# Tokens, meta tokens, norm gains and a low rank weight laid out by partition before the launch, in a two-block transformer kernel

## What is computed

```
h = concatenate([meta, x], axis=1)                   # 16 + 256 tokens, 1024 wide
hn = rmsnorm(h, norm_mix[0])
h = h + gla_mixer(hn, gla_w_in, gla_w_a1, gla_w_a2, gla_b_a, gla_g_out, gla_w_out)
...                                                  # ffn, sparse attention, ffn
h = concatenate([zeros, meta_2, x], axis=1)          # the second stack, x from the first
```

## Time and profile before

| | us |
|---|---|
| median of 3 runs | 1350.13 (1350.03 to 1351.98) |
| the profiled execution | 1350.41 |
| its span, first to last instruction | 1348.6 |
| TensorE matmul busy in it | 1341.5 (99%) |
| TensorE weight load busy | 1281.3 (95%) |
| VectorE, ScalarE, GpSimd busy | 1009.2, 708.1, 296.7 |
| DMA, mean over the span | 170 GB/s |

### The profile page before, as it was taken

One profiled execution on the slowest core, in us unless ns is written; L12 is line 12 of the kernel. 1 busy time (PEld: TensorE's weight loads), 2 busy tenths in 40 slices (PEclk: granted clock), 3 DMA queues, 4 the chain that ended last, 5 costly groups with the idle time before them and its releaser, 6 DMA issues.

```text
span 1348.6 us, 24729 instructions
## 1 busy us (share of the span) xinstructions
PE 1341.5 (99%) x9873; PEld 1281.3 (95%) x9873; DVE 1009.2 (75%) x1613; ACT 708.1 (53%) x1167; POOL 296.7 (22%) x313
## 2 busy tenths in 40 slices
PE   9999999999999999999999999999999999999998
PEld 9999999999999888899999999999999999988886
DVE  6788766655997988888877876766557885898843
ACT  7565544444756555544444664544445565655543
POOL 1136000023152000132366744000022533120000
PEclk9999999999999999999999999999999999999999
DMA  8334665665443655555443455555554653566552
GB/s 280 126 125 157 193 188 186 194 187 161 135 159 128 218 190 191 170 200 187 160 139 126 154 187 160 187 168 177 172 172 145 191 157 127 168 202 192 193 183 77
DMA packets 220457, 229.72 MB, mean 170 GB/s; under 512 B 13664, under 2 KB 207704, under 8 KB 220344
## 3 DMA queue, kind: packets, MB, share of 16 engines
q1 hardware_dynamic: 219232, 226.24, 52.7%
q10 hardware_dynamic: 1112, 1.90, 0.6%
HBM read 226.80 MB, written 1.33 MB: 169 GB/s over the span
## 4 chain that ended last, share of the span: by engine, by line
PE 99%; DMA 0%; issue 0%; DVE 0%; ACT 0%; ACTq 0%; DVEq 0%
PE ps L605 28%; PE ps L603 21%; PE ps L601 20%; PE ps L598 14%; PE ps L1163 2%; PE ps L1162 2%; PE ps L1164 2%; PE ps L664 1%; PE ps L666 1%; PE ps L665 1%; PE ps L932 1%; PE ps L802 1%; PE ps L1007 1%; PE ps L790 0%; PE ps L1095 0%; PE ps L889 0%
## 5 line engine op out<-in xcount | busy, mean ns | idle before, releaser
L1204 ACT ACTIVATE uh<-raw 128x1024 fp32r<-128x1024 f32 (+4 forms) x452 | 446.7, 999 | 433.5 <-PE ps L605 372.9
L1800 DVE TENSOR_TENSOR ul<-raw,uh 128x1024 fp32r<-128x1024 f32 (+3 forms) x448 | 528.3, 1187 | 130.0 <-PE ps L605 82.1
L605 PE MATMUL ps<-xx,ul 128*128 128x272 f32 (+1 forms) x2136 | 603.1, 282 | 0.0
L601 PE MATMUL ps<-xx,uh 128*128 128x272 f32 (+1 forms) x1448 | 419.1, 289 | 0.0
L603 PE MATMUL ps<-xx,uh 128*128 128x272 f32 (+1 forms) x1448 | 414.9, 287 | 0.0
L605 PEld LDWEIGHTS ps<-xx,ul 128*128 128x128 f32 x2136 | 402.3, 188 | 0.0
L601 PEld LDWEIGHTS ps<-xx,uh 128*128 128x128 f32 x1448 | 272.4, 188 | 3.0 <-issue 1.7
L603 PEld LDWEIGHTS ps<-xx,uh 128*128 128x128 f32 x1448 | 272.6, 188 | 0.8
L605 PE MATMUL ps<-aa,ul 128*128 128x272 f32 (+1 forms) x920 | 260.7, 283 | 0.0
L598 PE MATMUL ps<-xx,uh 128*128 128x512 f32 x704 | 244.7, 393 | 0.0
L601 PE MATMUL ps<-aa,uh 128*128 128x272 f32 (+1 forms) x788 | 226.7, 288 | 0.0
(11 more groups left out here) (343 smaller groups left out, 1645.6 us busy)
## 6 DMA issues: line engine op xcount, KB each, us to landing
raw<-in_ffn_w SPq DMA_DIRECT2D x62, 1024.0 KB, 5.3
raw<-in_ffn_w_in SPq DMA_DIRECT2D x44, 1024.0 KB, 5.2
raw<-in_ret_w_in SPq DMA_DIRECT2D x24, 1024.0 KB, 5.1
raw<-in_ffn_w_out SPq DMA_DIRECT2D x16, 1024.0 KB, 5.7
raw<-in_gla_w_in SPq DMA_DIRECT2D x11, 1024.0 KB, 5.1
raw<-in_ret_w_o SPq DMA_DIRECT2D x8, 1024.0 KB, 5.2
raw<-in_dsa_w_in SPq DMA_DIRECT2D x7, 1024.0 KB, 5.5
raw<-in_ffn_w_out SPq DMA_DIRECT2D x8, 768.0 KB, 5.0
```

What stands on the lines that cost most here:

```text
L601: e.matmul(in_turns(ps[:, 0:n1 - n0]), hi[:, k, :], in_turns(x.hi[:, k0 + j, n0:n1]), start=first and j == 0, stop=False)
L605: i = e.matmul(in_turns(ps[:, 0:n1 - n0]), lo[:, k, :], in_turns(x.hi[:, k0 + j, n0:n1]), start=False, stop=last and j == len(ks) - 1)
L1204: i = e.activation(unit_hi(u)[:, :, cols], a, ACT.Copy)
L1800: i = e.tensor_tensor(unit_lo(u)[:, :, cols], a, unit_hi(u)[:, :, cols].bitcast(F32), ALU.subtract)
```

## The change

The host now hands over arrays that are already laid out by partition: `tokens` ([128, 8, 272], meta tokens and `x` together), `meta_2` ([128, 8, 16]), `gla_w_a1` ([128, 8, 16]) and all `gains` ([128, 120]). The transposes, the staging buffers and the copies out of PSUM go. `h` is loaded directly, in four pairs of chunks: 0 and 1 by SP behind the low rank weight, 2 and 3 by SP behind the first half of slab 1, 4 to 7 by ScalarE's queue. The squares for the norm are taken in channel order, on GpSimd for chunks 0 to 3 and on ScalarE for 4 to 7; VectorE adds them up in one reduction, TensorE sums over partitions (`total`), now after five chunks of unit 2, ScalarE takes the root, VectorE the reciprocal. Ten warm-up matmuls run instead of six. Cut to its core:

```diff
 TensorE
-            warm(5)
-            ps = small("gain0", "D")
...
-                for n in (1, 2):
-                    i = turned(ps, k, n)
...
+            warm(10)
...
-            chunk(("gk", 1), "D", x, 0, T)
-            ps = small(("n", 0), "D")
-            w.wait_ge(s_diag, 3)
-            done(e.matmul(ps[:, 0:T], ones[:, :], g_diag[:, P - NM:3 * P], start=True, stop=True), ("n", 0))
+            gk1 = lin.take(w, ("gk", 1), "D")
+            product(gk1, x, 0, T, 0, True, False, range(5))
+            total(("n", 0), "A", s_first, 1, ssq[0], T)
+            product(gk1, x, 0, T, 5, False, True, range(5, KC))
...
-            product(gk2, x, 0, T, 0, True, False, range(4))
-            ps = small("gain1", "D")
-            w.wait_ge(s_row, 16 * (len(ROWS) - 1))
-            done(e.transpose(ps[:, 0:NG], grow[0:NG, :], ident[0:NG, 0:NG]), "gain1")
+            product(gk2, x, 0, T, 0, True, False, range(6))
             gate(0)
             gate(1)
...
-                        i = e.transpose(ps[:, k * NM:(k + 1) * NM], r_stage[0:NM, k * P:(k + 1) * P], ident[0:NM, 0:NM])
 ScalarE
+            e.dma_start(gains[:, 0:NG], A["gains"]).then_inc(s_gain, 16)
+            for j in (2, 3):
+                e.dma_start(h[:, 2 * j:2 * j + 2, :], A["tokens"][:, 2 * j:2 * j + 2, :]).then_inc(s_h[j], 16)
             w.wait_ge(s_const, 4)
             table(ACT.Sqrt)
+            hi()
+            w.wait_ge(s_gain, 16)
+            for k in range(KC):
+                x_hi(0, k, 0, G(gcol["norm_mix"] + k), (s_h[k // 2], 16))
             w.wait_ge(s_gz, 1)
             for r in (0, 32):
                 e.dma_start(g_a2[r:r + 16, :], A["gla_w_a2"][0]).then_inc(s_a2, 16)
...
+            hi_in_halves()
             hi()
+            for j in (2, 3):
+                e.activation(tmps[:, 2 * j - 4:2 * j - 2, :], h[:, 2 * j:2 * j + 2, :], ACT.Square).then_inc(s_sq[0], 1)
             hi()
+            root(("n", 0), float(D), eps6, rbc[:, :])
             table(ACT.Exp)
 VectorE
+            lo()
             for k in range(KC):
+                x_lo(0, k, 0, G(gcol["norm_mix"] + k))
             lo()
             lo()
+            w.wait_ge(s_ssq[0], 7)
+            w.wait_ge(s_sq[0], 2)
+            e.tensor_reduce(ssq[0][:, :], tmps[:, 0:5, :].rearrange("p k n -> p n k"), AX, ALU.add).then_inc(s_first, 1)
             lo()
...
             w.wait_ge(*aux.emptied(("n", 0)))
+            e.reciprocal(rbc[:, :], rbc[:, :]).then_inc(s_first, 1)
 GpSimd
+            for k in range(4):
+                src, sq = h[:, k, :], total if k == 0 else tmp[5] if k == 1 else sqt[:, k % 2, :]
+                w.wait_ge(s_h[k // 2], 16)
+                e.tensor_tensor(sq, src, src, ALU.mult).then_inc(s_ssq[0], 1)
+                if k:
+                    w.wait_ge(s_ssq[0], 2 * k)
+                    e.tensor_tensor(total, total, sq, ALU.add).then_inc(s_ssq[0], 1)
 SP
-            e.dma_start(cst[:, 0:P], A["c_tab"][:, 0:P]).then_inc(s_id, 16)
...
                     if s == units[HALVED][0]:
                         e.dma_start(to[:, 0:4, :], src[:, 0:4, :]).then_inc(s_raw_half, 16)
+                        e.dma_start(h[:, 2:4, :], A["tokens"][:, 2:4, :]).then_inc(s_h[1], 16)
                         to, src = to[:, 4:8, :], src[:, 4:8, :]
                     e.dma_start(to, src).then_inc(s_raw[s % NRAW], 16)
+                if s == 0:
+                    e.dma_start(h[:, 0:2, :], A["tokens"][:, 0:2, :]).then_inc(s_h[0], 16)
```

More of the change, by code:

```diff
@@ L506, in build @@
         s_raw_half, s_hi_half, s_lo_half = sem("s_raw_half"), sem("s_hi_half"), sem("s_lo_half")
[L508 to L511, removed]
+        s_const, s_tab, s_gain, s_meta, s_first, s_a2 = (
+            sem(n) for n in ("s_const", "s_tab", "s_gain", "s_meta", "s_first", "s_a2"))
+        s_h = [sem(f"s_h{i}") for i in range(KC // 2)]
         s_gx = sem("s_gx")
@@ L973, in _ @@
             rows("d", y_dsa, [5, 6, 7])
-            def new_meta(t):
-                if t == 8:
-                    ps = small("meta", "A")
-                    w.wait_ge(s_rstage, 16)
-                    for k in range(KC):
-                        i = e.transpose(ps[:, k * NM:(k + 1) * NM], r_stage[0:NM, k * P:(k + 1) * P], ident[0:NM, 0:NM])
-                    done(i, "meta")
-            ffn(1, NM, new_meta)
+            ffn(1, NM, lambda t: None)
             x = norm_x(4)
@@ L1206, in hi, with hi_in_halves @@
                 u += 1
-            def hi_in_halves(between):
+            def hi_in_halves():
                 nonlocal u
@@ L1566, in new_meta @@
                 if t == 5:
-                    e.dma_start(r_stage[0:NM, :], A["meta_2"]).then_inc(s_rstage, 16)
+                    w.wait_ge(s_xl[2], KC)
+                    w.wait_ge(s_ssq[2], 15)
+                    e.dma_start(h[:, :, 0:NM], A["meta_2"]).then_inc(s_meta, 16)
                     for hd in range(2):
                         e.dma_start(r_dk[hd], A["c_dec"][:, hd * DW:(hd + 1) * DW]).then_inc(s_dk[hd], 16)
-                if t == 9:
-                    w.wait_ge(*aux.full("meta"))
-                    e.activation(h[:, :, 0:NM], aux.bank("meta")[:, 0:KC * NM].rearrange("p (k n) -> p k n", k=KC),
-                                 ACT.Copy).then_inc(aux.empties("meta", "A"), 1)
             ffn(1, NM, new_meta)
@@ L2242, in meta_square @@
                 if t == 12:
-                    w.wait_ge(*aux.emptied("meta"))
+                    w.wait_ge(s_meta, 16)
                     e.tensor_tensor(r_sqm, m, m, ALU.mult).then_inc(s_metasq, 1)
@@ L2802, in bias_part @@
                     [LB, NR], [NR * (LB + 1), 8], [1, NKEY[b]]])).then_inc(s_bias, 16)
-            e.dma_start(cst[:, 0:P], A["c_tab"][:, 0:P]).then_inc(s_id, 16)
-            for half in range(2):
-                cols = slice(half * 512, half * 512 + 512)
-                for b in range(2):
-                    e.dma_start(g_stage[:, 1 + b, cols], A["x"][0, b * P:(b + 1) * P, cols]).then_inc(s_x[half], 16)
             for s, (loads, made) in enumerate(slabs):
                 if s == NRAW:
-                    for r0, n, src in rows[1:]:
-                        e.dma_start(grow[r0:r0 + n, :], src).then_inc(s_row, 16)
-                    e.dma_start(cst[:, P:C_END], A["c_tab"][:, P:C_END]).then_inc(s_tab, 16)
+                    e.dma_start(cst[:, :], A["c_tab"]).then_inc(s_tab, 16)
                 if s >= NRAW:
@@ L2894 @@
     named = [(n, np.ascontiguousarray(inputs[n])) for n in _INS]
+    given = {n: np.asarray(a) for n, a in inputs.items()}
+    gains = np.concatenate([given[n].reshape(-1, P) for n, _ in ROWS], axis=0)
+    named += [("tokens", in_columns(np.concatenate([given["meta"], given["x"][0]], axis=0).T)),
+              ("meta_2", in_columns(given["meta_2"].T)), ("gla_w_a1", in_columns(given["gla_w_a1"][0])),
+              ("gains", np.ascontiguousarray(gains.T))]
     for name, a in named + [("c_tab", tab), ("c_hot", hot), ("c_dec", dec)]:
```

104 lines of the change are left out of this document (17 added, 87 removed).

## The result

| | before | after |
|---|---|---|
| median | 1350.36 us (20 runs, 1350.03 to 1351.98) | 1352.51 us (20 runs, 1351.72 to 1354.23) |
| profiled execution, its span | 1350.41, 1348.6 | 1352.3, 1350.5 |

The ratio is 1.0017, with a 95% interval of 1.001 to 1.0023: the changed kernel is 2.1 us slower, which is real, and less than the 0.2% named ahead. The forecast was 1351.8 us, 1.7 over the three runs known then, and no change that can be told.

The account below looks back on a forecast made before the run. Bound: gapless TensorE, so only unit 1's start and TensorE's later work count. 1350.41 + 1.5 (start) - 0.8 (work removed) + 1.0 (clock) = 1352.1, less 0.28 to the median: 1351.8 us; 8-in-10 range 1349.0 to 1354.4.

Parts of the forecast that it names:

- The bound: TensorE works gapless from 4.95 us; only unit 1's start and TensorE's work after it can move the end.
- TensorE's own work, -0.8: Dropping the eight `meta_2` transposes saves 0.7 us and the transpose of the other gains 0.1, in gapless work.
- Landing 8.5: Token chunks 2 and 3 land at 8.5 us as two queues share the DMA engines; bounds 7.0 and 9.0.
- Six rests, 3.9: VectorE's rests of six chunks before unit 1 take 0.65 us each beside GpSimd's squares and additions, 3.9 us together.
- Unit 1 at 13.6: TensorE starts unit 1 at 13.6 us against 12.14, +1.5; bounds 10.8 and 15.0.
- The clock, +1.0: TensorE waiting for chunks before unit 1 loses 1.0 us to the lower clock level; bounds 0 and 2.5.
- that speaks for staying, if it has come by then: At the program's end 3.5 us without a matmul still showed clock 1.00, so the upper level may outlast TensorE's early wait.
- ScalarE hidden: Before unit 1, ScalarE's copies, two DMA issues and half copy end at 12.0 us, before VectorE at 12.9.
- The reduction, 1.8: VectorE's reduction of five times 272 elements for the norm takes 1.8 us; sum ready 3.9 after unit 1's start, needed at 5.0.
- The third rival: The norm's chain outlasts its thin cover and TensorE waits 1 us at the sum or gate: 1352.8 us, chance 0.09.
- From unit 3 on the same distances as before: TensorE's matmuls from unit 3 on stand as far apart as in the kernel before, one sign of the forecast.
- the prediction's own test: A difference arising after 30 us, other than at the meta tokens, would prove the whole account wrong.

Follow-up runs that it names:

- e1_tokens_first: Changed kernel with SP loading token chunks 2 and 3 ahead of the half slab instead of behind it: 1352.18 us, ratio 1.0012.
- e2_fill: Changed kernel with small matmuls on ones between the chunks of unit 0, nothing else changed: 1351.77 us, ratio 1.0007.
- e8_meta2_only: Kernel before with one part of the change alone, `meta_2` laid out and its eight transposes gone: 1349.58 us, ratio 0.9993.
- e3_pool_later: Changed kernel with GpSimd squaring chunks 2 and 3 only after VectorE has made all eight rests: 1353.61 us, ratio 1.002.
- e5_first_fill: Changed kernel with token chunks 2 and 3 ahead of the half slab and small matmuls between unit 0's chunks: 1351.47 us, ratio 1.0004.
- e7_act_fill: e6_squares_on_act with small matmuls between the chunks of unit 0: 1350.28 us, ratio 0.9999.
- e9_adds: e7_act_fill with four additions on VectorE instead of one reduction, and no additions on GpSimd: 1349.54 us, ratio 0.9996.
- e12_adds_rests_first: e9_adds with unit 4's rounding ahead of the root on ScalarE and its rest ahead of the reciprocal on VectorE: 1348.68 us, ratio 0.9988.
- e11_fill_rests_first: e5_first_fill with unit 4's rounding ahead of the root on ScalarE and its rest ahead of the reciprocal on VectorE: 1350.49 us, ratio 1.0.
- e6_squares_on_act: Changed kernel with chunks 2 and 3 loaded first, squares 0 to 3 on ScalarE, sum and gates asked for later: 1350.47 us, ratio 1.0004.
- e4_slab_first: Changed kernel with both halves of slab 1 ahead of token chunks 2 and 3: 1354.54 us, ratio 1.0029.

## Why the prediction was right

- **The bound** was read rightly: the time moved with the start of unit 1 behind gapless work and with TensorE's own work, and little else.
- **TensorE's own work, -0.8**: measured 0.79 at the meta tokens, and 0.79 again where it was the only edit. The 0.1 for the transpose of the gains is there too: the lag falls from +2.41 to +2.30 once both kernels are past the first gate products, and the same 0.11 shows in e1_tokens_first and e2_fill. Together 0.90 for 0.8.
- **Landing 8.5**: 8.2. The two queues shared the DMA engines, at 350 to 400 GB/s from 6 us on. The rule of the Trainium skill (DMA: Bandwidth & Descriptors, Queues, rings and completion order), that the engines go round between the queues, agrees: by my estimate a queue served alone would have landed near 7.0, and ScalarE's last pair, on the other queue, landed at 6.9 ahead of it.
- **Six rests, 3.9**: 3.96. Right in sum by luck, with a wrong working. GpSimd's squares took 0.64 to 0.84, not the 1.63 of the earlier trace rows, so it was done with its last addition at 11.6 us and not beside all six: three rests took 0.87 to 1.00, three 0.49 to 0.50. The contention per rest was larger than my 0.65, and shorter. The Trainium skill (GPSIMD Engine Reference, Specifications) names the shared interfaces; here a rest took 0.4 to 0.5 us longer while GpSimd squared or added, which agrees; beside its memset, at 11.82, a rest took 0.49. The first of the six took 0.50 too, though it lay across the end of a square and the start of an addition.
- **Unit 1 at 13.6**: 13.38. Its first distance, 0.1 longer than before, was not in the sum.
- **The clock, +1.0**: 1.06 in the trace, and 1.0 between the lags of e2_fill and the changed kernel. The size, a choice between 0 and 2.5, was right by luck, and the ground for it was not. The sentence "that speaks for staying, if it has come by then" failed: the level had come by 6 us and fell while TensorE had a chunk now and then. The earlier trace rows showed an idle end of program, and were a poor neighbour. The upper bound was one execution's too: e8_meta2_only has the upper level 3.6 us earlier with the same instructions.
- **ScalarE hidden**: yes, but the two DMA issues did not "stand behind" its last chunk. They ran at 8.23, beside the activations, and delayed none. The sum for this path also left out the last chunk's own 0.4: with its terms the half copy would end at 12.4, not 12.0, still ahead of VectorE.
- **The reduction, 1.8**: 2.62. Mis-sized: line 1891 reduces pairs from PSUM, 1.35 ns for each element read, this one five rows of 272 lying apart in SBUF, 1.93. Which of the differences costs it is not shown. The cover held, with 1.7 us to spare at the sum (ready 17.7, asked for at 19.39). The third rival needed about that much to come true, and in e3_pool_later it did.
- **"From unit 3 on the same distances as before"**: wrong by 0.2 us. I counted TensorE's cover for root and reciprocal, and not what was queued behind the waiting instructions on ScalarE and VectorE: a rounding and a rest that free a ring slot. By the prediction's own test ("a difference that arises after 30 us other than at the meta tokens would prove the whole wrong") this speaks against it; it was a term left out of the sum, small here because the start was late enough to hide most of it. In e5_first_fill, with an earlier start, the same term was 1.4 us.

Term by term the forecast was +1.5 - 0.8 + 1.0 = +1.7, and the trace has +1.24 + 0.11 - 0.90 + 1.06 + 0.20 and 0.17 of drift, +1.88. The late start and the clock's fall, the two costs that the prediction named, are the two that were paid. That the sum came so close is partly luck, as said of its terms. (The range's upper end adds up to 1354.3, not 1354.4.)

What stays open: when the clock falls and returns. With the same warm-up matmuls in unit 0, the profiles of e5_first_fill, e7_act_fill, e9_adds and e12_adds_rests_first show no fall once the upper level has come (by the distances at 6.0, 7.0, 4.4 and 7.0 us), that of e11_fill_rests_first shows 0.50 from 9 to 11 us. The mean granted clock of each execution says roughly how often; it is rough because the time ahead of the first recorded change counts as 1.00, rightly or not. It is 0.995 to 0.997 in 17 of the changed kernel's 20 executions and 0.996 or 0.997 in all eleven of e1_tokens_first, but 0.999 or 1.000 in all eleven of e5_first_fill, whose only difference from e1_tokens_first is the small matmuls, and in ten of eleven of e11_fill_rests_first, whose profiled one has 0.998. So they keep the level up most of the time. In e6_squares_on_act, where chunks come every 0.4 us, it stayed up in the profile without them. In four experiments' profiles (e1, e2, e3 and e4) TensorE also has a wait of 0.9 us on its own issue near 747 us, where the changed kernel's has 0.2. It adds 0.6 to their lag; what it comes from is open, and the lags are read ahead of it.

## What to carry to other kernels

When an edit puts a wait on an engine, list what is queued behind it, up to the instruction that frees a buffer, and follow that buffer through the DMA queue to the next wait: here one pair of instructions behind a root and a reciprocal cost up to 1.4 us 25 us later, on an engine whose wait was not in sight of it. On this kernel, bound by one gapless engine, work taken off that engine showed in full in its lag (0.79 for 0.7 forecast), while time won at its start was taken back by its clock or by the next chain. Holding the helper engine back only moved its contention: ask which of its neighbours has slack. And profile the same start twice before you read half a microsecond from one trace.

## What the chip did that I had not expected

- The clock fell to its lower level with TensorE still given matmuls, two or three in a microsecond, and came back at 15.7, within gapless work. The runs of a kernel spread very differently, and keeping TensorE at work doesn't explain it: 2.5 us for the changed kernel (20 runs), 0.6 for e12_adds_rests_first (11), but 2.2 and 3.3 for e5_first_fill and e9_adds, with the same small matmuls.
- The page gives a granted clock of 1.00 for stretches at the start in which matmuls run at half rate: in e4_slab_first unit 1's neighbours are 0.22 us apart up to 17.1 us:
```profile
16.42 0.43 PE L593 MATMUL ps<-xx,uh 128*128 128x272 f32 x1
16.64 0.43 PE L595 MATMUL ps<-xx,ul 128*128 128x272 f32 x1
```
  The distance of neighbours is the safer reading.
- A reduction over five rows of 272 that lie apart takes 2.55 to 2.67 us, 1.9 ns for each element read; the addition of 544 elements takes 0.72.
- VectorE's rest of 1024 weights takes 1.21 us alone and 1.79 beside GpSimd's square; its half 0.69 and 1.13. GpSimd's square of 272 took 0.64 beside the activations and 1.62 beside that rest.
